# A delta rule's work laid out anew between VectorE and ScalarE, and q's sums of squares taken on TensorE without transposes

## The reference

```python
qkv = jax.nn.silu(causal_depthwise_conv(qkv, w_conv_qkv[i]))
q, k, v = jnp.split(qkv, 3, axis=-1)
q, k, v = l2norm(heads(q)), l2norm(heads(k)), heads(v)   # x * rsqrt(sum(x*x) + EPS)
...
A = jnp.einsum('bhnid,bhnjd->bhnij', kb, k) * decay * strict
T = lax.linalg.triangular_solve(eye + A, ...)
u = jnp.einsum('bhnij,bhnjd->bhnid', T, v * beta[..., None])
w = jnp.einsum('bhnij,bhnjd->bhnid', T, kb * jnp.exp(gc)[..., None])
qk = jnp.einsum('bhnid,bhnjd->bhnij', q, k) * decay
q_dec = q * jnp.exp(gc)[..., None]
k_end = k * jnp.exp(g_last[..., None] - gc)[..., None]
def step(Sst, inp):                                       # S0 = 0
    v_new = u_n - jnp.einsum('bhid,bhde->bhie', w_n, Sst)
    o = jnp.einsum('bhid,bhde->bhie', qd_n, Sst) + jnp.einsum('bhij,bhje->bhie', qk_n, v_new)
    Sst = Sst * jnp.exp(gl_n)[..., None, None] + jnp.einsum('bhid,bhie->bhde', ke_n, v_new)
```

## Time and profile before

| | us |
|---|---|
| median of 3 runs | 2368.41 |
| lowest and highest | 2366.63, 2372.14 |
| the profiled execution's time | 2367.83 |
| its span | 2366.2 |
| TensorE busy | 2340.8 |
| VectorE busy | 1627.0 |
| ScalarE busy | 1174.6 |

### The profile page before, as it was taken

The page is one execution under the profiler, slowest core; times in us unless marked ns, Lnnn a source line. Parts: engine busy times, 40 slices in busy tenths (PEclk is TensorE's granted clock), DMA queues, the critical chain, the costliest instruction groups (busy, mean ns, idle before and its releaser), DMA issues.

```text
span 2366.2 us, 35125 instructions
## 1 busy us (share of the span) xinstructions
PE 2340.8 (99%) x13692; PEld 1923.5 (81%) x13692; DVE 1627.0 (69%) x2147; ACT 1174.6 (50%) x1554; POOL 233.7 (10%) x410
## 2 busy tenths in 40 slices
PE   8999999999999999999999999999999999999998
PEld 7888888777777777788888888888888888888887
DVE  5899999878787878656665756666666544555565
ACT  5555555576454545444555654535353444443443
POOL 3000000112121213011000101001010000000100
PEclk9999999999999999999999999999999999999999
DMA  7566666766555658488655557776776755676673
GB/s 252 187 213 204 204 196 228 234 205 232 179 187 179 191 175 286 152 289 284 217 194 194 193 173 240 229 229 233 225 239 223 247 192 185 230 260 190 223 252 125
DMA packets 239247, 506.87 MB, mean 214 GB/s; under 512 B 15065, under 2 KB 15938, under 8 KB 238210
## 3 DMA queue, kind: packets, MB, share of 16 engines
q1 hardware_dynamic: 214898, 418.57, 53.8%
q0 software_dynamic: 24208, 86.31, 11.4%
HBM read 464.45 MB, written 40.39 MB: 213 GB/s over the span
## 4 chain that ended last, share of the span: by engine, by line
PE 65%; DVE 1%; DMA 1%; ACT 0%; issue 0%; POOL 0%; DVEq 0%; ACTq 0%
PE acc L2604 58%; PE acc L2624 2%; PE acc L2639 1%; PE aux L2666 1%; PE aux L2811 0%; DMA delta_branch_spill<-ol 0%; PE aux L3112 0%; DMA r1l<-delta_branch_spill 0%; PE aux L3117 0%; PE aux L3017 0%; PE aux L2652 0%; PE acc L3017 0%; PE aux L2917 0%; PE aux L2804 0%; PE aux L2904 0%
## 5 line engine op out<-in xcount | busy, mean ns | idle before, releaser
L1644 DVE TENSOR_TENSOR w_lo<-raw,w_hi 128x1024 fp32r<-128x1024 f32 x790 | 962.4, 1222 | 653.7 <-ACT w_hi L960 642.0
L960 ACT CAST w_hi<-raw 128x1024 fp32r<-128x1024 f32 x790 | 824.3, 1049 | 980.7 <-PE acc L2604 938.7
L2604 PE MATMUL acc<-w_hi,r1h 128*128 128x512 f32 x1828 | 722.3, 395 | 3.0 <-DVE w_lo L1644 1.9
L2604 PE MATMUL acc<-w_lo,r1h 128*128 128x512 f32 x1828 | 709.3, 388 | 0.0
L2604 PE MATMUL acc<-w_hi,r1l 128*128 128x512 f32 x1828 | 708.5, 388 | 0.0
L2604 PE MATMUL acc<-w_hi,r2h 128*128 128x512 f32 x1208 | 472.2, 391 | 0.2 <-DVE r2l L1738 0.2
L2604 PE MATMUL acc<-w_hi,r2l 128*128 128x512 f32 x1208 | 470.2, 389 | 0.0
L2604 PE MATMUL acc<-w_lo,r2h 128*128 128x512 f32 x1208 | 470.1, 389 | 0.0
L2604 PEld LDWEIGHTS acc<-w_hi,r1h 128*128 128x128 f32 x1828 | 343.3, 188 | 81.6 <-DVE w_lo L1644 6.3
L2604 PEld LDWEIGHTS acc<-w_hi,r1l 128*128 128x128 f32 x1828 | 343.3, 188 | 72.0
L2604 PEld LDWEIGHTS acc<-w_lo,r1h 128*128 128x128 f32 x1828 | 343.6, 188 | 65.4
(11 more groups left out here) (507 smaller groups left out, 1589.1 us busy)
## 6 DMA issues: line engine op xcount, KB each, us to landing
raw<-in_w_in SPq DMA_DIRECT2D x263, 1024.0 KB, 5.1
raw<-in_w_out SPq DMA_DIRECT2D x32, 1024.0 KB, 5.2
raw<-in_w_br_b SPq DMA_DIRECT2D x16, 1024.0 KB, 5.3
raw<-in_w_br_a SPq DMA_DIRECT2D x16, 1024.0 KB, 7.5
raw<-in_w_ple_gate SPq DMA_DIRECT2D x16, 1024.0 KB, 5.1
raw<-in_w_o_mla SPq DMA_DIRECT2D x16, 1024.0 KB, 5.1
raw<-in_w_o_conv SPq DMA_DIRECT2D x16, 1024.0 KB, 5.2
raw<-in_w_q_b SPq DMA_DIRECT2D x8, 1024.0 KB, 5.1
```

What stands on the lines that cost most here:

```text
L960: nc.scalar.copy(w_hi[:, h % HL, 0:n], raw[:, k % RAW, x * HALF:x * HALF + n]).then_inc(hi_ready, 1)
L1644: V.tensor_tensor(w_lo[:, h % HL, 0:n], raw[:, k % RAW, x * HALF:x * HALF + n], w_hi[:, h % HL, 0:n].bitcast(F32), ALU.subtract).then_inc( ...
L2604: ins = T.matmul(acc[:, s, x, 0:n], a[:, kt0 + k, xs_], w[:, h % HL, at], start=start and k == 0 and m == 0, stop=stop and k == kts - 1 an ...
```

## The change

- q's transposes go for i = 1 to 3. Instead ScalarE squares qT into cy in slot 16, and behind slot 17 (Q_SUM) TensorE sums it by ones: four products, one for each block of 32 tokens of a tile, each 32 columns of ones against 256 columns, into partitions 32b to 32b + 31 of bank 3. VectorE picks the diagonal of each 32 x 32 block by a product with ident_b and a reduction, both over 256 columns, in slot 18. GpSimd's factor becomes 0.25 x 2048.
- The waits of slot 16 on TensorE and the one for tok_ready ahead of the first new state are dropped; the new products wait for tok_ready and w_ready.
- kbe and ke move from VectorE (slot 2) to ScalarE (slots 3 and 5), as 8 and 10 scalings of one head and tile each. kbe and ke rows that nothing reads are left out.
- w of the first chunk is not computed: 4 of 16 products, and half of the first wT copy. qdT skips the first chunk and is made in slot 11.
- VectorE's state updates and the last update of the inverse (uinv) move into `delta_first`, ahead of that slot's w_lo.
- k's convolution, silu and transposes come one slot later (i = 1 to 3), k's transposes in i = 0 too.

```diff
-OWN = ((8, 0, 12, (12, 15), 15, 16), (16, 0, 20, (20, 22), 23, 24), (24, 0, 31, (27, 29), 30, 31))
-OWN_FIRST = ((8, 9, 10, (11, 15), 16, 19), (16, 20, 21, (22, 24), 25, 27), (24, 26, 27, (27, 29), 30, 31))
+OWN = ((8, 0, 12, (12, 15), 15, 16), (16, 0, 21, (21, 23), 24, 25), (24, 0, 31, (27, 29), 30, 31))
+OWN_FIRST = ((8, 9, 10, (11, 15), 16, 19), (16, 20, 21, (22, 24), 25, 28), (24, 26, 27, (27, 29), 30, 31))
+Q_SUM = 17
...
             def own(ph, hl, i, first):
+                if not first and hl == Q_SUM - 1:
+                    act.wait_ge(sem("s_ready"), i * 2 + 1)
+                    sig(A(cy[:].rearrange("p h n -> p (h n)"), qT[:].rearrange("p h n -> p (h n)"), ACT.Square), "tok_ready", i * 2 + 1)
...
-                for n, r in enumerate(CHUNK_ROWS):
-                    act.wait_ge(sem("uw_done"), dv(4, TT + n + 1))
-                    sig(nc.scalar.copy(wT[:, :, :, r].rearrange("p t h i -> p (t h) i"), X[:, 2 + n].rearrange("p (m i) -> p m i", i=SEQ_CHUNK)),
-                        "w_ready", dv(2, n + 1))
+                act.wait_ge(sem("uw_done"), dv(4, TT + 1))
+                sig(nc.scalar.copy(wT[:, 1, :, CHUNK_ROWS[0]], X[:, 2, TOK:2 * TOK].rearrange("p (h i) -> p h i", i=SEQ_CHUNK)), "w_ready", dv(2, 1))
+                act.wait_ge(sem("uw_done"), dv(4, TT + 2))
+                sig(nc.scalar.copy(wT[:, :, :, CHUNK_ROWS[1]].rearrange("p t h i -> p (t h) i"), X[:, 3].rearrange("p (m i) -> p m i", i=SEQ_CHUNK)),
+                    "w_ready", dv(2, 2))
...
+                if hl == 3:
+                    act.wait_ge(sem("cols_ready"), dv(1, 1))
+                    for x, rows in ((0, CHUNK_ROWS[1]), (1, slice(0, P))):
+                        for h in range(GH):
+                            c.inc(A(kbe[rows, x, h], ktok[rows, x, h], ACT.Copy, scale=dcol[rows, 4, x, h:h + 1]))
+                if hl == 5:
+                    for x in range(TT):
+                        for dst, src, hs in PLACES:
+                            for h in range(hs.start, hs.stop):
+                                if x == 0:
+                                    c.inc(A(ke[dst, x, h], ktok[src, x, h], ACT.Copy, scale=dcol[src, 5, x, h:h + 1]))
+                                elif src.start == 0:
+                                    to = slice(dst.start, dst.start + SEQ_CHUNK)
+                                    c.inc(A(ke[to, x, h], ktok[CHUNK_ROWS[0], x, h], ACT.Copy, scale=dcol[CHUNK_ROWS[0], 5, x, h:h + 1]))
+                    c.wait()
+                    act.sem_inc(sem("k_scaled"), 1)
...
+                    if hl == Q_SUM + 1 and n == 0 and not tap0:
+                        dve.wait_ge(sem("tok_tr"), i * 2 + 1)
+                        c.link(V.tensor_tensor(xs_b, X[:, 3, 0:TOK].rearrange("p (m i) -> p m i", i=BLK), rep(ident_b[:], TC2), ALU.mult))
+                        sig(V.tensor_reduce(dcol[:, 8].rearrange("p t h -> p h t"), xs_b.rearrange("p (h t) i -> p h t i", h=GH), AX.X, ALU.add),
+                            "qk_square", i * 2 + 1)
...
-                if hl == 15:
-                    dve.wait_ge(sem("egc_landed"), dv(32, 32))
-                    sig(V.tensor_tensor(flat(qdT), flat(qT), flat(egc_rep), ALU.mult), "qdT_ready", dv(1, 1))
+                if hl == 11:
+                    dve.wait_ge(sem("egc_landed"), dv(32, 32))
+                    sig(V.tensor_tensor(qdT[:, :, SEQ_CHUNK:], qT[:, :, SEQ_CHUNK:], egc_rep[:, :, SEQ_CHUNK:], ALU.mult), "qdT_ready", dv(1, 1))
...
+                    if hl == Q_SUM and n == 0 and i:
+                        pe.wait_ge(sem("tok_ready"), i * 2 + 1)
+                        pe.wait_ge(sem("w_ready"), i * 2)
+                        squares = cy[:].rearrange("p h (x b i) -> p b (h x) i", x=TT, i=BLK)
+                        for b in range(len(BLOCKS)):
+                            ins = T.matmul(X[BLOCKS[b], 3, 0:TOK], ones_mean[:, 0:BLK], squares[:, b], start=True, stop=True)
+                        ins.then_inc(sem("tok_tr"), 1)
-                    if hl == back and n < 2:
+                    if hl == back and n < 2 and (n or i == 0):
                         pe.wait_ge(sem("s_ready"), i * 2 + (n + 1))
+                        if i:
+                            pe.wait_ge(sem("qk_square"), i * 2 + 1)
...
                         for n, r in enumerate(CHUNK_ROWS):
+                            if (x, n) == (0, 0):
+                                continue
                             ins = T.matmul(X[:, 2 + n, m * SEQ_CHUNK:(m + 1) * SEQ_CHUNK], kbe[r, x, h], uinv[r, x, h], start=True, stop=True)
...
-                            if n == 0 and own_tr:
-                                pe.wait_ge(sem("tok_ready"), own_tr)
...
-                    if hl == 16:
-                        pe.wait_ge(sem("u_ready"), dv(2, 2))
-                        pe.wait_ge(sem("w_ready"), dv(2, 2))
```

More of the change, by code:

```diff
@@ L803, in _ @@
             ln_out(1)
[L804 removed]
+            columns_q(0, 0.25)
             ln_out(2)
@@ L1171, in own @@
             def own(ph, hl, i, first):
+                if not first and hl == Q_SUM - 1:
+                    act.wait_ge(sem("s_ready"), i * 2 + 1)
+                    sig(A(cy[:].rearrange("p h n -> p (h n)"), qT[:].rearrange("p h n -> p (h n)"), ACT.Square), "tok_ready", i * 2 + 1)
                 for n, (evac, _, pad, (_, conv_end), silu, back) in enumerate(OWN_FIRST if first else OWN):
-                    if hl == back + 1 and n < 2:
+                    if hl == back + 1 and n < 2 and (n or first):
                         act.wait_ge(sem("tok_tr"), i * 2 + (n + 1))
@@ L1978, in own @@
                         sig(V.scalar_tensor_tensor(flat((qT, kT)[n]), flat(cth), 1.0, flat(cy), ALU.add, ALU.mult), "s_ready", i * 2 + (n + 1))
-                    if hl == back + 2 and n < 2:
+                    if hl == Q_SUM + 1 and n == 0 and not tap0:
[3 more added lines that the diff above has]
+                            "qk_square", i * 2 + 1)
+                    if hl == back + 2 and n < 2 and (n or tap0):
                         dve.wait_ge(sem("tok_ready"), i * 2 + (n + 1))
@@ L1991, in delta_first @@
             def delta_first(hl, dv):
[L1992 to L2051, removed]
-                if hl == 9:
-                    dve.wait_ge(sem("qk_done"), dv(1, 1))
-                    c.link(V.tensor_tensor(th(decT), th(decT), rep(tri_c[:], TC2), ALU.mult))
-                    scores = X[:, 1].rearrange("p (t h i) -> p t h i", t=TT, h=GH)
-                    for dst, src, hs in PLACES:
-                        ins = V.tensor_tensor(qkT[dst, :, hs], scores[dst, :, hs], decT[src, :, hs], ALU.mult)
-                        if src is not PLACES[-1][1]:
-                            c.inc(ins)
-                    sig(ins, "qkT_ready", dv(1, 1))
-                if hl == 15:
-                    dve.wait_ge(sem("egc_landed"), dv(32, 32))
-                    sig(V.tensor_tensor(flat(qdT), flat(qT), flat(egc_rep), ALU.mult), "qdT_ready", dv(1, 1))
-                if V_CONV[0] <= hl <= V_CONV[1]:
-                    short_conv(hl, 2, *V_CONV, dv(3, 3), 0)
-                def v_silu(x):
-                    dve.wait_ge(sem("cth_ready"), dv(3, 3))
-                    at = slice(x * P, (x + 1) * P)
-                    v = flat(cth).rearrange("p (h n) -> p h n", h=GH)[:, :, at]
-                    sig(V.scalar_tensor_tensor(v, v, 1.0, cy[:, :, at], ALU.add, ALU.mult), "v_ready", dv(2, x + 1))
-                if hl in (10, 11):
-                    v_silu(hl - 10)
@@ L2093, in delta @@
                             c.wait()
+                for n in range(1, NCH):
+                    x, (rows, out_rows) = n // 2, scan_rows(n)
+                    if hl == 17 + 2 * n:
+                        dve.wait_ge(sem("scan_done"), dv(SCAN, 2 * n))
+                        for h in (0, GH // 2):
+                            v = us[out_rows[h], x, h:h + GH // 2].rearrange("p h d -> p (h d)")
+                            ins = V.tensor_tensor(v, v, X[out_rows[h], 0, h * DK:(h + GH // 2) * DK], ALU.subtract)
+                            if h == 0:
+                                c.inc(ins)
+                        sig(ins, "scan_ready", dv(SCAN, 2 * n))
+                        c.wait()
@@ new lines, in delta_first @@
+                if hl == 4 + 2 * LEVELS:
+                    dve.wait_ge(sem("lx_done"), dv(LEVELS, LEVELS))
+                    sig(V.tensor_copy(xs_b, blocks(0)), "xs_ready", dv(LEVELS, LEVELS))
+                if hl == 5 + 2 * LEVELS:
+                    dve.wait_ge(sem("ly_done"), dv(LEVELS, LEVELS))
+                    for b in BLOCKS[::2]:
+                        ins = V.tensor_scalar(th(uinv)[b, :, LATE], blocks(0)[b], -1.0, None, ALU.mult)
+                        if b is BLOCKS[0]:
+                            c.inc(ins)
+                    sig(ins, "inv_ready", dv(LEVELS, LEVELS))
+                    c.wait()
```

55 lines of the change are left out of this document (49 added, 6 removed).

## The result

The changed kernel takes 2372.86 us (median of 12 runs) where the kernel before, on the same chip, takes 2368.22 (12 runs). The ratio is 1.0019, 95% interval 1.0012 to 1.0027: slower by 0.2%, where 0.3% faster was forecast and 2365.5 was the top of the range. One of the twelve runs took 5420 us, which no profile here explains; the ratio leaves it out. The profiled execution took 2371.83 us, span 2370.2, 4.0 more than the span of before.

What follows compares the result with a forecast made beforehand. TensorE, busy 99% of the span, was taken to bound the kernel. 5.65 - 1.35 + 1.93 + 3.2 = 9.4 us gained, 2.2 given back, 7.2 net: median 2361.2 us, range 2357.5 to 2365.5.

Steps and rivals of the forecast that it cites:

- no DMA is added or moved past one: GpSimd and the DMA queues: GpSimd only changes a factor, waiting for the same semaphores; charged at nothing.
- An edit is worth what it takes from TensorE's list: Whole kernel: it ends when TensorE's list is done, so an edit gains what it takes from that list or TensorE's idle time.
- w: Slot 15, four groups: eight of 32 records fewer for w's products, 0.48 us each group, 1.93 us gained.
- slot 6: Four groups: ke on ScalarE delays w_hi, w_lo and xs, so TensorE waits 0.56 us each, 2.2 us lost.
- the ones: Slot 17, groups 1 to 3: q's four products with ones take 0.45 us each, 1.35 us lost.
- q: Slot 16, groups 1 to 3: q's transposes go, with the idle time ahead of them; 5.65 us gained.
- rival (b): w: a lone half of a pair takes what the pair took, so dropping four saves nothing; 2363.1 us, chance 0.12.
- The waits expected to go: TensorE's waits for uinv (1.0 us), the state update (0.8) and group 0's k transposes (1.4): 3.2 us gained.
- Rival (d): Slot 6: ke's scalings take far above 0.294 us each, four crossing partitions; at 0.65 each, 2375.5 us; chance 0.06.
- Slot 17: New place of slot 16's wait: ScalarE's Square is in time by 0.2 us, so charged 0.
- Rival (a): Slot 17: Square 1 us late in three groups, and slot 6's wait 0.9 us instead of 0.56; 2365.5 us, chance 0.15.

Runs made afterwards that it cites:

- repaired versions: Changed kernel with the last reload ahead of the spills, plus kbe and ke back on VectorE (2364.26, again 2364.68 us) or ke split over slots 5 and 7 (2364.94 us).
- the two repairs: Each alone on the changed kernel: kbe and ke back on VectorE, 2367.95 us; the last reload ahead of the spills, 2368.35 us.

## Why the prediction was wrong

**The step that failed** is the sentence "no DMA is added or moved past one", charged at nothing. It looked at the order of the instructions on GpSimd's queue, which indeed is the same, and not at when the queue gets there, nor at whom its last transfer serves. In the earlier trace rows the reload has no wait, since it was 0.7 us early. The change makes TensorE 1.4 us earlier and GpSimd's spills 1.9 later, since more of its small operations meet a w_lo. Cost: 2.3 us, and 1.5 on the clock in one of the two profiles. In the profiles, whatever else TensorE gains ahead of YB ends in this wait too: in six of them, with TensorE asking between 934.8 and 939.6 us, the reload landed between 940.3 and 941.7. In the medians it is less: moving the reload ahead of the spills gives 3.8 us, and the gain of kbe and ke on VectorE stands with or without it. "An edit is worth what it takes from TensorE's list" holds here only as far as the next transfer that comes by its own clock. Between the 7.2 us forecast as gained and the 4.0 us lost in the profile lie 11.2, of which the reload and the clock behind it are 3.8, the largest part but a third of it. The others: w_lo after 1500 us 2.0, w 1.9, "issue" 1.8, slot 6 1.1, the ones 0.35, and 0.5 elsewhere, some 11.5 in all; neither "issue" nor w_lo is a term of the forecast.

**q** was right: 5.65 us went, and no step is left in slot 16. The ones cost 0.57 instead of 0.45 each, since small products follow them, not big ones: 1.7 for 1.35.

**w** was wrong by its whole 1.93 us; rival (b), put at 0.12, is what happened. The argument from the k by k products compared weights of 64 with those of 128 columns, but the k by k products come in pairs as well (of output partitions, not of rows), and a lone half was in no row. What does free time is a pair gone: 24 to 16 records, 0.88 us. The Trainium skill (TensorE: Matmul & The Clock Gate, "Part 3: Packing small matmuls — row/col tiling") states that products in distinct row groups run side by side. By that rule nothing is freed; the trace agrees, with 1.92 us for 24 records and 1.93 for 32.

**The waits expected to go** went: uinv, state and kT, 3.2 us.

**Slot 6** was the right mechanism at half its size: 1.1 us where 0.56 stood, in three groups and, where the reload doesn't cover it, the fourth. The term mis-sized is the scaling: ten took 3.75 us to the next w_hi, some 0.35 each, against 0.294 taken from those of otok. The whole bound of 1.5 each wasn't reached. Rival (d)'s formula, 0.56 + 10 x (t - 0.294), gives the 1.1 us with t at 0.35, but its cause isn't there: crossing partitions costs nothing to speak of. By the code not four but six of the ten cross; by shape, four that cross (64 x 128) take 0.391 us each by themselves and two that stay (128 x 128) 0.395. (The t at which (d) eats the whole gain is 0.47 by that formula, not 0.49; nothing hangs on it.)

**Slot 17** was charged at 0 and cost 0: in group 1 the squares are done at 632.39 and TensorE asks at 632.87. Rival (a) didn't come, and its margin is 0.5 us where 0.2 was said, still thin: with TensorE 0.9 us quicker in slot 15 it is there, 0.3 us in two groups.

**The forecast sum** was 7.2 us. The version with ke split and the reload ahead shows 7.4 in TensorE's steps in its profile, made up differently (no slot-6 wait, no w gain). The medians of the repaired versions gain 2.8 to 3.0. That execution is the fastest of its eleven; what lies between it and the median isn't in a trace.

**Left open:** the "issue" stall of 0.7 to 1.7 us in the middle of a row of 64 small products with tinv. It is in eight of the eleven profiles of the changed kernel, plain or edited (in the plain one at 728.28 us, in group 2; in the version with kbe and ke on VectorE and the reload ahead at 949.95), and in neither of the kernel before. It isn't in those with k's slots as before, with the reload ahead alone, and with ke split and the reload ahead. Nothing in the views says what TensorE waits for. Nor is it settled why the version with the reload issued early, but landing at the same time, gained 3.5 us, why the gains of the two repairs add up, nor what decides whether the waits for w_lo after 1500 us come.

## What to carry to other kernels

When the bounding engine gets quicker, list the transfers that it meets later, with their landing and the moment at which it asks for each: a transfer without a wait in the profile may have a slack of 0.7 us, and then it is the new bound. Look at what stands ahead of its issue on its queue, and at what stands ahead of it on the DMA engines; here an issue 12 us earlier changed nothing in the landing until it passed the spills that filled them. Two small products in different rows of the array were paid by the pair here, so count the pairs that go, not the products.

## What the runs showed that was not expected

- A 512 KB reload took 4.8 us from issue to landing at the end of a burst, and 17.3 when it was issued 12 us earlier behind 1 MB of spills: landing time, not latency, was what stayed.
- After waits of 2.07, 2.34, 2.35, 5.4 and 5.6 us TensorE's clock fell to its lower level (big products 0.43 us apart) in five profiles, and not after one of 2.48. For the waits of 2 to 2.5 us nothing seen here tells which.
- A scaling of 128 columns by a column on ScalarE, over 64 or 128 partitions, costs 0.35 us in a row of ten, whether it stays in its partitions or crosses them, and 0.32 in the row of eight for kbe (2.57 us with its end).
- An operation of 8 columns on GpSimd took 0.2 us, and 0.7 to 1.3 when it began while VectorE made a w_lo, which is 1.22 us long: it ended with it. Under VectorE's update of ol from PSUM it took 0.20.
